# The packet size of layer 1's copied keys in a decoder trunk that moves its caches beside the compute

## The reference, cut to what matters

```
kk = jnp.concatenate([k_buf, k], axis=1)
vv = jnp.concatenate([v_buf, v], axis=1)
o = dilated_attention(q, kk, vv, k_buf.shape[1])
new_k = kk[:, -n_keep:]
new_v = vv[:, -n_keep:]
```

## Time and profile before

| what | us |
|---|---|
| median of 3 runs | 405.16 (402.5 to 406.25) |
| the profiled execution, its own time | 401.24 |
| its span, first to last instruction | 399.4 |
| TensorE busy in the span | 344.5 |
| VectorE busy in the span | 231.7 |

### The profile page before, as it was taken

One profiled execution on the slowest core, in us unless ns is written; L12 is line 12 of the kernel. 1 busy time (PEld: TensorE's weight loads), 2 busy tenths in 40 slices (PEclk: granted clock), 3 DMA queues, 4 the chain that ended last, 5 costly groups with the idle time before them and its releaser, 6 DMA issues.

```text
span 399.4 us, 4715 instructions
## 1 busy us (share of the span) xinstructions
PE 344.5 (86%) x1546; PEld 270.8 (68%) x1546; DVE 231.7 (58%) x524; ACT 99.4 (25%) x234; POOL 53.5 (13%) x102
## 2 busy tenths in 40 slices
PE   2799699999798869899949999997979877989990
PEld 1588488887576646688738888885647654658880
DVE  1604679889858974610132589847994997441110
ACT  3300114433523314210020021541352222230011
POOL 8400500060003300033000410006000030000000
PEclk9789989999879889999969999998978988989997
DMA  7999999999999999999999999999999999999993
GB/s 288 416 416 402 420 416 415 419 418 410 417 421 418 394 413 397 391 417 400 399 419 419 418 395 415 418 418 419 418 422 416 406 365 344 372 390 390 384 387 130
DMA packets 45157, 158.10 MB, mean 396 GB/s; under 512 B 6820, under 2 KB 20062, under 8 KB 45134
## 3 DMA queue, kind: packets, MB, share of 16 engines
q0 software_dynamic: 14976, 87.28, 54.1%
q10 hardware_dynamic: 14394, 41.52, 26.2%
q1 hardware_dynamic: 15764, 29.02, 19.5%
HBM read 141.58 MB, written 104.42 MB: 616 GB/s over the span
## 4 chain that ended last, share of the span: by engine, by line
SPq 33%; PE 23%; DMA 21%; DVE 9%; ACTq 5%; issue 3%; ACT 3%; DVEq 0%
SPq L469 23%; DMA kg<-in_cache_k_win 10%; DMA out<-kg 10%; PE pj L668 9%; SPq L449 8%; PE pj L811 8%; ACTq L848 3%; DVE yc L1250 2%; SPq L523 2%; DMA cst<-in_const 2%; PE ptr L593 1%; DVE ssc L1194 1%; DVE tok L1188 1%; PE psc L740 1%; PE psc L593 1%
## 5 line engine op out<-in xcount | busy, mean ns | idle before, releaser
L668 PE MATMUL pj<-hT,wt 128*128 128x264 f32 x800 | 198.4, 407 | 5.4 <-DVE hT L1108 5.3
L668 PEld LDWEIGHTS pj<-hT,wt 128*128 128x128 f32 x800 | 159.3, 202 | 38.5 <-issue 10.1
L1250 DVE SCALAR_TENSOR_TENSOR yc<-u_ext,par,yc 128x256 f32<-128x256 f32 x180 | 77.3, 481 | 3.5 <-DVE mix L1143 0.8
L811 PE MATMUL pj<-mix,wt 128*128 128x264 f32 x256 | 61.1, 395 | 0.0
L811 PEld LDWEIGHTS pj<-mix,wt 128*128 128x128 f32 x256 | 49.2, 195 | 8.4
L582 POOL DMA_DIRECT2D out<-in_cache_v_win x48 | 26.2, 555 | 155.3 <-issue 155.3
L582 POOL DMA_DIRECT2D out<-in_cache_k_win x48 | 26.0, 550 | 115.8 <-issue 115.8
L1320 DVE TENSOR_TENSOR xT<-xT,pj 128x264 f32<-128x264 f32 x16 | 6.9, 429 | 55.2 <-PE pj L811 55.2
L925 ACT ACTIVATE ex<-pj 128x264 f32<-128x264 f32 x22 | 8.6, 391 | 77.7 <-issue 44.2
L1188 DVE TENSOR_TENSOR tok<-kg,qb 128x1536 f32<-128x1536 f32 x10 | 17.6, 1758 | 6.3 <-DMA kg<-in_cache_k_win 5.9
L1134 DVE SCALAR_TENSOR_TENSOR u_ext<-ex,pj 128x256 f32<-128x256 f32 x6 | 2.5, 422 | 29.1 <-ACT ex L925 29.1
(11 more groups left out here) (175 smaller groups left out, 324.3 us busy)
## 6 DMA issues: line engine op xcount, KB each, us to landing
wt<-in_w_tiles ACTq DMA_DIRECT2D x62, 512.0 KB, 31.3
out<-in_cache_k_win POOLq DMA_DIRECT2D x24, 1080.0 KB, 70.0
out<-in_cache_v_win POOLq DMA_DIRECT2D x24, 1080.0 KB, 79.5
out<-in_cache_k_win POOLq DMA_DIRECT2D x8, 1200.0 KB, 80.3
out<-in_cache_v_win POOLq DMA_DIRECT2D x8, 1200.0 KB, 77.3
out<-in_cache_k_win POOLq DMA_DIRECT2D x16, 432.0 KB, 73.5
out<-in_cache_v_win POOLq DMA_DIRECT2D x16, 432.0 KB, 79.2
kg<-in_cache_k_win SPq DMA_DIRECT2D x32, 144.0 KB, 32.3
```

What stands on the lines that cost most here:

```text
L668: last = nc.tensor.matmul(pj[n % RING][:, 0:T], wt[:, g % WRING, k, :], hT[:, k, :], start=(k == 0), stop=(k == KD - 1))
L811: last = nc.tensor.matmul(pj[n % RING][:, 0:T], wt[:, g % WRING, k, :], mix[:, k, :], start=(k == 0), stop=(k == KD - 1))
L1250: last = V.scalar_tensor_tensor(out=yc[:, t, 0:SEQ], in0=x_w, scalar=par[:, ROW_CW + w * CT + t:ROW_CW + w * CT + t + 1], in1=yc[:, t, 0:S ...
```

## The change

Layer 1's copied keys are cut as its values are: a block of 15 rows goes in three packets of 7680 B and not in four of 5760 B. Bytes, addresses, transfers and their order stay.

```
-DEEP_BYTES = {"k": (DEEP_STEP - 1) * C_ATT * 4 // 4, "v": (DEEP_STEP - 1) * C_ATT * 4 // 3}
+DEEP_BYTES = (DEEP_STEP - 1) * C_ATT * 4 // 3
...
-                        size = DEEP_BYTES[kind]
+                        size = DEEP_BYTES
```

## The result

The changed kernel took 410.62 us (median of 5 runs, 409.16 to 414.05) against 404.75 us (median of 5, 402.5 to 406.25). The ratio is 1.0153, 95% interval 1.0119 to 1.0186: 5.9 us slower, where 11 were forecast. The profiled execution of the changed kernel took 414.05 us with a span of 412.2 us, that is 12.8 us more than the span before.

A forecast was written before the change was run, and what follows sets the result against it. Full DMA queues served in packet turns were taken to bound the kernel; 11.2 us for longer turns less 0.2 us fixed cost gave 412.2 us profiled and 416.0 us as median, range 409 to 420.5.

The forecast's parts named there:

- Turns, one packet each: DMA engines serve one packet from each of three queues in turn; a round from 50 to 75 us takes 0.384 us.
- Longer turns: Layer 1's larger key packets lengthen each round by 42 ns, making weights and gathers up to some 11 us late.
- Early weights: Up to about 50 us the compute goes by rounds of weight transfers, so it runs 4.4 us late.
- Layer 0's keys: Their gather lands 7.9 us late, at 90.0 us, making the compute 6.8 us late.
- Layer 0's values: Their gather lands 11.1 us late, at 157.1 us, making the compute 10.1 us late.
- Layer 1's keys: Their gather, already waited for, comes at 282.9 instead of 271.74 us; the compute behind is 11.2 us late.
- Layer 1's values: Landed by 331.2 and used at 335.20 us before; both move by 11.2 us, adding nothing new.
- Fixed cost: Overhead of the 768 packets removed from layer 1's key copies: 0.2 us saved, bounds 0 to 2.7 us.
- so the lateness reaches the end: Behind layer 1's keys come arithmetic and output projection at TensorE's speed, so all 11.2 us stay.
- that cover at the end is now 11 us wide and buys nothing: At the end, copies finish at the same clock time while compute is later; SyncE had waited only 1.0 us for them.
- half is absorbed: Added round time lies in packet gaps, or compute behind layer 1's keys wins some back: about 410.8 us, chance 0.16.
- only the total counts: Emptying of the queues sets the end, so equal bytes give no slowdown: 404.9 us, chance 0.07.

The follow-up runs named there:

- the dose: Layer 1's keys in two packets of 11520 B instead of four, values in three, against the kernel before: 423.14 us, ratio 1.0522.
- k3v4: Layer 1's keys in three packets and values in four, against the kernel before's four and three: 399.42 us, ratio 0.9938; run again, 400.17 us.
- the repeats: The changed kernel, unedited, run twice more against the kernel before: 406.03 us, ratio 1.0094, and 407.88 us, ratio 1.0098.

## Why the prediction was right, and where it was off

Right were the sign, the mechanism and its place. A step at a time:

- *Turns, one packet each.* Shown by equal counts in three kernels of the dose (1041, 925, 807), and by k3v4, in which only the count of packets had been put back.
- *Longer turns.* 42 ns a round forecast, 432 - 384 = 48 ns in the first profile and about 45 in the second.
- *Early weights.* The compute was to be 4.4 us late by layer 0's keys. Without its wait for them VectorE would have started at 87.95 (90.72 - 2.77) and 87.58 us, 4.7 and 4.3 us after 83.24.
- *Layer 0's keys*: 90.0 forecast, 90.72 and 89.11. *Layer 0's values*: 157.1 forecast, 157.44 and 156.61. *Layer 1's keys*: 282.9 forecast, 286.74 and 281.26.
- *Layer 1's values* were to keep 4 us of slack. They didn't: L740 waited 0.69 and 1.62 us for them, and already 3.56 us in the second profile of before. That slack was the luck of one profile. In the first pair it changed nothing in the sum; in the second the lateness fell there from 9.9 to 7.1 us.
- *Fixed cost.* 0.2 us taken; 1.4 us with the copies alone, inside the bounds of 0 to 2.7.

Mis-sized was the **sum**: 11.0 us forecast, 5.9 measured (and 3.8 and 3.9 in the repeats, by their ratios), mainly through one step: "so the lateness reaches the end", and with it "that cover at the end is now 11 us wide and buys nothing". I had looked at SyncE's wait of 1.0 us for the last copy and taken the compute for what ended last. The view had another row, 5.5 us for stores of `vg`, and 10.7 us lay between the last L1320 and the end, of which the outputs need 5.3. So 5.4 us of lateness were free in that profile. The runs without the six last copies bear it out: the kernel before gains 5.6 us, and where nothing is hidden the gap is 10 to 13 us, about as the term was sized. In the second pair of profiles only 0.9 us were free at the end, and the rest was lost at layer 1's values and behind them. How the two parts share in the medians is not shown run by run.

That the first pair differs by 12.8 us, near the 11.0 forecast for the profiled execution, is luck: its compute was 7.0 us later than forecast, 18.2 against 11.2, and the end hid 5.4. The measured median of 410.62 us is that of the rival "half is absorbed" (410.8). Its first mechanism, overlap of packets, the runs don't show: a round grew by 45 to 48 ns, more than the 42 taken. Its second, that the compute behind the keys wins some back, shows in the second pair only, with 3.5 us. And the rival "only the total counts" had right what ended the kernel before in its first profile: transfers, and not the compute.

## What to carry to other kernels

Where several queues keep the DMA engines full, the engines serve them packet by packet, so the packet size of a transfer that nobody waits for sets the speed of the transfers that somebody does wait for. Work out how much further the background queue gets in as many turns, and follow the lateness from gather to gather. Then look at both ends, the compute's last step and the last landing: what is late in one is free up to the gap between them. The best split of those tried was keys in three and values in four packets; in its two profiles the last L1320 starts 8.2 and 12.4 us ahead of the span's end, so by the 5.3 us that the outputs need, 2.9 and 7.1 us of the compute's lateness would be free there.

## What the runs showed of the hardware that was not expected

The copies alone moved 8.17 MB in 25 us (327 GB/s), while three queues together moved 10.39 MB in the same stretch (416 GB/s), and the busy share of the 16 engines read 100.2 and 102.5%. A packet was counted 1.002 x 400 / 1547 = 259 ns alone for 5281 B, 49 ns per 1000 B, against 38.6 beside the two others. A busy share of an engine is thus no measure of the bytes that it moves. It does not follow that one queue alone leaves the engines room. A copied byte is read from memory (HBM) and written back to it, a weight is only read, and by the pages of the profiles the memory traffic of the two kernels is nearly the same; first the kernel before, then the copies alone with four packets:

```profile
HBM read 141.58 MB, written 104.42 MB: 616 GB/s over the span
```

```profile
HBM read 87.27 MB, written 87.27 MB: 634 GB/s over the span
```

Whether the single queue or the memory traffic holds the copies to 327 GB/s, no run here tells.
